# Cross attention's output projections as seven half-size products per weight unit, their weight sums on GpSimd

## The reference, cut to what matters

```
def memory_cross_attention(h, mem, g_mem, w_q, w_kv, w_o):
    ...
    p = jax.nn.softmax(sc, axis=-1)                                   # 4 heads of 256
    o = jnp.einsum("bhqk,bkhd->bqhd", p, v.astype(jnp.float32))
    return o.reshape(b, s, D_MODEL) @ w_o                             # 256x1024 by 1024x1024
h = h + memory_cross_attention(...)
h = h + squared_relu_mlp(rmsnorm(h, ...), ...)
```

## Time and profile before

| what | value |
| --- | --- |
| time, median of three runs | 1585.96 us (1585.59 to 1586.88) |
| the profiled execution: its time | 1585.89 us |
| its span, first to last instruction | 1584.1 us |
| TensorE busy | 1431.3 us, 90% |
| VectorE, ScalarE, GpSimd busy | 765.3, 313.5, 29.9 us |
| granted TensorE clock, mean | 0.962 |

### The profile page before, as it was taken

One profiled execution on the slowest core, in us unless ns is written; L12 is line 12 of the kernel. 1 busy time (PEld: TensorE's weight loads), 2 busy tenths in 40 slices (PEclk: granted clock), 3 DMA queues, 4 the chain that ended last, 5 costly groups with the idle time before them and its releaser, 6 DMA issues.

```text
span 1584.1 us, 23677 instructions
## 1 busy us (share of the span) xinstructions
PE 1431.3 (90%) x10066; PEld 1119.1 (71%) x10066; DVE 765.3 (48%) x1567; ACT 313.5 (20%) x774; POOL 29.9 (2%) x51
## 2 busy tenths in 40 slices
PE   9999999999999999999999999999988566657657
PEld 8779989998888799899988888888743112113113
DVE  6637617879667556178797678823320000000000
ACT  1332022220024520122200343332211000000000
POOL 0000000000002000000000012000000000000000
PEclk9999999999999999999999999999999888787889
DMA  9525415776434054157665204346899999999998
GB/s 394 236 80 192 181 54 192 287 279 265 164 143 181 33 209 164 54 208 289 262 266 225 82 1 132 118 131 262 354 394 426 426 426 429 427 426 428 426 427 346
DMA packets 47625, 396.53 MB, mean 250 GB/s; under 512 B 16416, under 2 KB 20256, under 8 KB 22688
## 3 DMA queue, kind: packets, MB, share of 16 engines
q1 hardware_dynamic: 46048, 393.53, 62.3%
q10 hardware_dynamic: 1472, 1.49, 0.3%
HBM read 392.38 MB, written 2.63 MB: 249 GB/s over the span
## 4 chain that ended last, share of the span: by engine, by line
PE 73%; DMA 22%; DVE 2%; SPq 1%; ACT 1%; issue 0%; ACTq 0%; DVEq 0%
PE pb L542 30%; DMA arena<-in_w_experts 21%; PE pb L1174 12%; PE pb L1138 11%; PE pb L642 7%; PE pb L1049 5%; PE pb L1082 3%; PE pb L1223 2%; SPq L1840 1%; PE pb L977 1%; PE pb L1249 1%; PE pb L713 1%; DMA cols<-in_cols 0%; ACT arena L1904 0%; DVE arena L3178 0%
## 5 line engine op out<-in xcount | busy, mean ns | idle before, releaser
L542 PE MATMUL pb<-hT,ring 128*128 128x256 f32 x768 | 173.2, 382 | 0.2 <-DVE arena L3300 0.2
L542 PEld LDWEIGHTS pb<-hT,ring 128*128 128x128 f32 x768 | 143.5, 190 | 24.9 <-issue 5.9
L542 PE MATMUL pb<-ring,hT 128*32 128x512 f32 (+2 forms) x704 | 110.4, 671 | 43.4 <-DMA ring<-in_w_experts 42.1
L3460 DVE SCALAR_TENSOR_TENSOR side<-side,pb 128x256 f32<-128x256 f32 x16 | 6.7, 422 | 267.3 <-ACT side L1904 267.3
L642 PE MATMUL pb<-arena,ring 128*128 128x256 f32 x512 | 118.2, 382 | 0.0
L1904 ACT ACTIVATE arena<-pb 128x512 f32<-128x512 f32 (+4 forms) x122 | 53.2, 458 | 305.3 <-PE pb L542 116.0
L542 PEld LDWEIGHTS pb<-ring,hT 128*32 128x32 f32 (+1 forms) x704 | 32.6, 131 | 110.1 <-issue 63.2
L642 PEld LDWEIGHTS pb<-arena,ring 128*128 128x128 f32 x512 | 94.9, 190 | 14.6 <-issue 2.9
L1904 ACT ACTIVATE side<-pb 128x256 f32<-128x256 f32 (+2 forms) x58 | 23.1, 407 | 402.1 <-PE pb L542 386.0
L542 PE MATMUL pb<-arena,hT 128*32 128x512 f32 x248 | 41.8, 796 | 34.6 <-DMA arena<-in_w_experts 21.5
L542 PE MATMUL pb<-ring,side 128*32 128x256 f32 (+1 forms) x608 | 45.2, 452 | 20.4 <-DMA ring<-in_w_experts 15.9
(11 more groups left out here) (489 smaller groups left out, 2498.1 us busy)
## 6 DMA issues: line engine op xcount, KB each, us to landing
ring<-in_w_dense SPq DMA_DIRECT2D x85, 2048.0 KB, 8.0
ring<-in_w_experts SPq DMA_DIRECT2D x54, 2048.0 KB, 45.3
arena<-in_w_experts SPq DMA_DIRECT2D x18, 2048.0 KB, 44.6
extra<-in_w_experts SPq DMA_DIRECT2D x9, 2048.0 KB, 45.3
cons<-in_w_experts SPq DMA_DIRECT2D x9, 1024.0 KB, 45.0
arena<-in_w_experts SPq DMA_DIRECT2D x9, 1024.0 KB, 41.9
ring<-in_w_experts SPq DMA_DIRECT2D x4, 1024.0 KB, 6.8
ring<-in_w_dense SPq DMA_DIRECT2D x2, 1536.0 KB, 6.4
```

Of the source, the lines that this page charges most:

```text
L542: return nc.tensor.matmul(o, l, r, start=st, stop=sp)
```

## The change

The output projection of both layers becomes seven half-size products for each of its two weight units. Weight sums T1 to T4 are made by GpSimd, into `extra` and `hT` (T3 in place in the unit), all eight from the moment that q1's last product is done. Row sums are made by VectorE: S3 behind head 2, S1, S2, S4 behind head 3. The products are issued by `out_product`: unit 0's 1 behind `turn(2)`, its 7 ahead of `turn(3)`, unit 1's 1 behind `turn(3)`, its 7 behind the last head, then 2 of both units, then 5, 6, 4, 3 of unit 0 and of unit 1. ScalarE copies product 1 of both units out of PSUM (`first_outs`) ahead of the last head's output. VectorE adds the products to quarters of the residual (`first_quarter`, `other_quarters`). The banks of q1's product become (6, 3, 7). `out_weight` is one subtraction of 128x1024 on GpSimd, `out_row` one sum or difference of 128x512 on VectorE, `first_quarter` adds product 2's bank to the residual's first quarter (128x256); `first_outs` is called in ScalarE's `attention` between the copies of the last head's `t` and `o`.

```
-                cross_columns(layer, "q1", (3, 6, 7), first_scores)
+                cross_columns(layer, "q1", (6, 3, 7), first_scores)
 
                 def all_copied():
-                    open_projection(f"xo{layer}_")
+                    for i in range(2):
+                        out_unit[layer, i] = take()
                     pe.wait_ge(v_ready, 8 * (layer + 1))
                     copied(pe, f"xq1{layer}_0", f"xq1{layer}_1")
 
-                attention(stage, all_copied, lambda h, part: between_cross(stage, h, part))
-                project(5)
+                attention(stage, all_copied, lambda h, part: between_cross(layer, h, part))
+                out_product(layer, 1, "7")
                 copied(pe, *outs(stage))
-                project(6)
-                project(7, final=True)
+                for i in range(2):
+                    out_product(layer, i, "2")
+                for i in range(2):
+                    for x in "5643":
+                        out_product(layer, i, x)
...
+            def out_product(layer, i, x):
+                w, u = out_unit[layer, i]
+                y = [[yT[:, HALF[b_], TOK[t]] for b_ in range(2)] for t in range(TT)]
+                place = {"1": 0, "2": 0, "4": 0, "5": 1, "3": 1, "6": 2, "7": 2}
+                lhs = {"1": w[:, HALF[0], FEAT[0]], "2": w[:, HALF[1], FEAT[0]], "3": w[:, HALF[1], FEAT[1]], "4": ow[i][2],
+                       "5": ow[i][0], "6": ow[i][1], "7": w[:, HALF[0], FEAT[1]]}
+                rhs = {"1": y[0][0], "2": y[0][1], "3": vh[3], "4": y[1][1], "5": vh[0], "6": vh[1], "7": vh[2]}
+                b = ((0, 4, 2), (3, 5, 1))[i][place[x]]
...
+                if x in "4567":
+                    pe.wait_ge(ow_ready, out_weights(layer, i, {"5": "T1", "6": "T2", "7": "T3", "4": "T4"}[x]))
+                if x in "3567":
+                    pe.wait_ge(oh_ready, out_rows(layer, {"5": "S1", "6": "S2", "7": "S3", "3": "S4"}[x]))
+                if x == "2":
+                    pe.wait_ge(op_copied, 2 * layer + i + 1)
+                if x == "4":
+                    pe.wait_ge(o2_read, 2 * layer + i + 1)
+                if x == "3":
+                    pe.wait_ge(o5_read, 2 * layer + i + 1)
+                for f in range(2):
+                    for k in range(4):
+                        o = side_ * S + f * P
+                        last = nc.tensor.matmul(pb[:, b, o:o + P], lhs[x][:, k, f * P:(f + 1) * P], rhs[x][:, k, :],
+                                                start=x in "157" and f == 0 and k == 0, stop=x not in "15" and k == 3,
+                                                skip_group_check=True)
+            def between_cross(layer, h, part):
+                at_ = {(2, 1): (0, "1"), (3, 0): (0, "7"), (3, 1): (1, "1")}
+                if (h, part) == (2, 1):
+                    copied(pe, *(f"o{FIRST_HEAD[f'xa{layer}'] + j}" for j in range(2)))
+                if (h, part) in at_:
+                    out_product(layer, *at_[h, part])
...
+        OUT_WEIGHTS = ((0, "T1"), (0, "T3"), (1, "T1"), (1, "T3"), (0, "T2"), (0, "T4"), (1, "T2"), (1, "T4"))
+            def out_weights_of(layer):
+                b, done = product_done["cross", layer, "q1", "3"]
+                pool.wait_ge(filled[b], done)
+                for i, which in OUT_WEIGHTS:
+                    out_weight(layer, i, which)
...
+            def first_outs(layer):
+                for i in range(2):
+                    b, m = product_done["out", layer, i, "1"]
+                    act.wait_ge(filled[b], m)
+                    fn(out_p1[i], pb[:, b, 0:S], ACT.Copy).then_inc(op_copied, 1)
...
+                    elif h == 2:
+                        copied(dve, *heads_out[0:2])
+                        out_row(layer, "S3")
+                attention(f"xa{layer}", behind_head)
+                copied(dve, *heads_out[2:4])
+                for which in ("S1", "S2", "S4"):
+                    out_row(layer, which)
+                for i in range(2):
+                    first_quarter(layer, i)
+                for i in range(2):
+                    other_quarters(layer, i, lambda c: col(f"mlp_norm{layer}", c))
-                add(f"xo{layer}_", lambda c: col(f"mlp_norm{layer}", c))
+            def other_quarters(layer, i, gain):
+                V.tensor_tensor(x11, x11, product_of(b, 0), ALU.add).then_inc(o5_read, 1)
+                link(V.tensor_tensor(u, u, product_of(b, 0), ALU.add))
+                link(V.tensor_tensor(x10, x10, u, ALU.add))
+                V.tensor_tensor(u, u, product_of(b, 1), ALU.add).then_inc(freed[b], 1)
+                link(V.tensor_tensor(x01, x01, u, ALU.add))
+                link(V.tensor_tensor(x11, x11, u, ALU.add))
+                for f, quarter, x, sign in ((0, x01, "4", ALU.subtract), (1, x10, "3", ALU.add)):
+                    V.tensor_tensor(quarter, quarter, product_of(b, 1 - f), sign).then_inc(freed[b], 1)
+                    V.tensor_scalar(raw(c), xT[:, c, :], gain(c), None, ALU.mult).then_inc(raw_ready, 1)
```

More of the change, by code:

```diff
@@ L426, in program, with out_weights, out_rows @@
         product_done, down_unit, value_unit, up_unit = {}, {}, {}, {}
+        out_unit = {}
+        OUT_WEIGHTS = ((0, "T1"), (0, "T3"), (1, "T1"), (1, "T3"), (0, "T2"), (0, "T4"), (1, "T2"), (1, "T4"))
+        OUT_ROWS = ("S3", "S1", "S2", "S4")
+        def out_weights(layer, i, which):
+            return 8 * layer + OUT_WEIGHTS.index((i, which)) + 1
+        def out_rows(layer, which):
+            return 4 * layer + OUT_ROWS.index(which) + 1
         summed = {}
@@ L676, in between_cd @@
                     project(c, 1 - part, first=c == 0)
[L678 to L683, removed]
+            def out_product(layer, i, x):
[5 more added lines that the diff above has]
+                rhs = {"1": y[0][0], "2": y[0][1], "3": vh[3], "4": y[1][1], "5": vh[0], "6": vh[1], "7": vh[2]}
+                side_ = x in "47"
+                name = f"xo{layer}_{i}_{place[x]}"
+                b = ((0, 4, 2), (3, 5, 1))[i][place[x]]
+                if x in "157":
+                    fill(name, b)
+                if x in "4567":
[14 more added lines that the diff above has]
+                                                skip_group_check=True)
+                mark(last, name, True, u if x == "3" else None)
+                product_done["out", layer, i, x] = (b, marks[b])
@@ L1858, in _, with out_weight @@
         def _(pool):
+            def out_weight(layer, i, which):
+                w, u = out_unit[layer, i]
+                w11, w12, w21, w22 = (w[:, HALF[a_], FEAT[b_]] for a_ in range(2) for b_ in range(2))
+                if which == "T1":
+                    pool.wait_ge(loaded[slot_of[u]], 16 * nth[u])
+                else:
+                    pool.wait_ge(ow_ready, out_weights(layer, i, "T2" if which == "T4" else "T1"))
+                if which == "T1":
+                    ins = nc.gpsimd.tensor_tensor(ow[i][0], w12, w11, ALU.subtract)
+                elif which == "T2":
+                    ins = nc.gpsimd.tensor_tensor(ow[i][1], w22, ow[i][0], ALU.subtract)
+                elif which == "T3":
+                    ins = nc.gpsimd.tensor_tensor(w12, w22, w12, ALU.subtract)
+                else:
+                    ins = nc.gpsimd.tensor_tensor(ow[i][2], ow[i][1], w21, ALU.subtract)
+                ins.then_inc(ow_ready, 1)
+            def out_weights_of(layer):
[3 more added lines that the diff above has]
+                    out_weight(layer, i, which)
+            out_weights_of(0)
             b, done = product_done["mixer", "qd", "3"]
@@ L2653, in cross, with behind_head @@
                 block_12(layer, "q0")
-                def last_queries(h):
+                heads_out = [f"o{FIRST_HEAD[f'xa{layer}'] + j}" for j in range(4)]
+                def behind_head(h):
                     if h == 0:
@@ new lines, in cross, with out_row @@
+                for i in range(2):
+                    first_quarter(layer, i)
+                for i in range(2):
+                    other_quarters(layer, i, lambda c: col(f"mlp_norm{layer}", c))
+            def out_row(layer, which):
+                y11, y12, y21, y22 = (yT[:, HALF[b_], TOK[t]] for t in range(TT) for b_ in range(2))
+                if which in ("S2", "S4"):
+                    dve.wait_ge(oh_ready, out_rows(layer, "S1" if which == "S2" else "S2"))
+                if which == "S1":
+                    ins = V.tensor_tensor(vh[0], y21, y22, ALU.add)
+                elif which == "S2":
+                    ins = V.tensor_tensor(vh[1], vh[0], y11, ALU.subtract)
+                elif which == "S3":
+                    ins = V.tensor_tensor(vh[2], y11, y21, ALU.subtract)
+                else:
+                    ins = V.tensor_tensor(vh[3], y12, vh[1], ALU.subtract)
+                ins.then_inc(oh_ready, 1)
```

32 lines of the change are left out of this document (29 added, 3 removed).

## The result

The change makes the kernel slower: 1596.39 us in the median of four runs (1594.63 to 1600.84) against 1586.28 (a fourth run of it joins the three above), ratio 1.0067, 95% interval 1.0056 to 1.0079. The forecast was 1581.6, its range 1580.0 to 1586.5; the time lies above it, beyond both slow rivals (1591.1 and 1593.8).

The account below looks back on a forecast made before the run. TensorE was taken to bound layers 0 and 1, DMA the end from us 1200. Per layer 2.63 + 0.53 - 0.06 - 0.45 - 0.5 = 2.15, two layers 4.3, from 1585.89 to 1581.6 us; range 1580.0 to 1586.5.

Parts of the forecast that it names:

- both slow rivals: Port held for both scalings of a pair: 1591.1 us, chance 0.13; GpSimd sums late for products: 1593.8, chance 0.03.
- the shared port: Heads 1 and 2: GpSimd sums delay VectorE's SBUF scalings 0.5 us each, 0.45 covered; loss 0.5 us per layer.
- the port is held, and both scalings of a pair are caught: Scalings 1 and 2 wait half a sum, then a whole one: 2.6 us lost per layer, 1591.1 us, chance 0.13.
- The sums' size: GpSimd's 128x1024 weight sums: 1.9 us each, the eighth ending near us 222; the tightest due time allowed 4.3 us.
- The products: Output projection: 14 half-size products of 1.79 us replace eight `project` calls, saving TensorE 2.63 us per layer.
- The bank swap: Behind q1's last product: transposes start at once, scores of head 2 come earlier; gain 0.53 us per layer.
- o1's copy: Product 1 of unit 0 waits for ScalarE's copy of o1 behind `weigh(1)`: loss 0.45 us per layer.
- The seam: From the last products to the MLP: VectorE's adds and scaled chunks are ready in time, nothing lost.
- Without the port: Rival: one-input scalings pass beside GpSimd's sums without waiting; gain 5.3 us, 1580.6 us, chance 0.25.
- the gain carries through to the end: The DMA-saturated stretch from us 1200 moves along with earlier savings; the opposing rival: 1585.9 us, chance 0.04.
- The chances: Summary for the whole kernel: faster by over 0.2% 0.66, within 0.19, slower 0.15.

Follow-up runs that it names:

- the PSUM kernel: The changed kernel with exponentials kept in PSUM, where VectorE's scalings read them, and GpSimd's sums unchanged: 1583.34 us, 0.9982 of the kernel before.
- The two kernels without it: The changed kernel with scalings reading PSUM (1583.34 us), and the changed kernel with all eight weight sums on VectorE (1582.95 us).
- the three kernels: Redundant waits added to the kernel with sums on VectorE (128: 1581.91 us; 256: 1580.19) and to the one with PSUM scalings (128: 1580.72).
- 64 waits: The changed kernel with sums on VectorE, plus 64 redundant waits in TensorE's stream: 1583.05 us, 0.9986 of the kernel before.

## Why the prediction was wrong

**The step that failed is the shared port.** It stood in the sum at 0.5 us per layer ("Sum 2 meets scalings 1 ...: 0.5 late. Sum 4 meets scalings 2: 0.5 late, of which 0.45 was idle"). Measured: 2.98 + 3.05 = 6.0 us of waits per layer, from pairs of scalings that took 3.81 and 3.88 instead of 0.62. That is the rival "the port is held, and both scalings of a pair are caught", given 0.13: mechanism, place and order were right, its price of 2.85 a head was 3.2. The four experiments above show it from four sides: it goes when the scalings leave SBUF as their input, it goes when the sums leave GpSimd, it comes with the sums alone, and it shrinks with the length of GpSimd's instruction.

The mistake lay in reading. There a VectorE operation with two inputs in SBUF took 0.84 for 0.69 beside a running GpSimd scaling, and I took this for the way of the port in general. The same form of VectorE operation, S3, took 2.84 beside a GpSimd sum. So the row was right and told of another GpSimd instruction, one with a single input; from it I chose a value between ends far apart, when the row met this case on neither engine. The second part I had argued and weighed too low: a pair of scalings with a gap between them gives a never-empty GpSimd queue the chance to take the port back, and it took it each time. (S3, issued next, waited for one sum only, which ended at 223.66: S3 ended at 224.22, and the last sum, started at 223.75 beside it, took 2.69.) The Trainium skill, page "SBUF — State Buffer", § Who interferes with whom, states the exclusion for the whole instruction. Beside sums this case's runs agree with it (1.47 and 2.42 us for scalings of 0.35, beside sums of 2.35), apart from the last 0.2 us or so of a sum: the scalings end 0.15 us behind it, and need 0.35 themselves. The 0.84 of the earlier trace rows, beside a one-input scaling, still stands against it, and no run looked at that pair.

**The sums' size.** 1.9 us forecast, 2.35 measured; a straight line through rows of 128 and 512 elements on fewer or as many partitions was too low by a fifth. The estimate of 2.25 from the Trainium skill, page "GPSIMD Engine Reference", § 3.1 (4497 ns for 2048 elements, halved), was nearer. They ended late enough to matter to nobody but the scalings: no product waited for a sum. Their length enters the price of the port, one sum for one scaling: with 1.9 us the same mechanism gave 2.85 a head, with 2.35 it gives half a sum and a whole one, 3.5, near the 3.2 measured.

**The products.** Right. Fourteen of 1.79 us each were forecast; eleven took 19.65, 1.786 each. (14 x 1.79 is 25.06 and not 25.0; at 1.786 it is 25.0.) Less work on TensorE by 2.6 us per layer is in the changed kernel too: waits grew from 0.61 to 6.3, 5.7; less 2.6 is 3.1, and each of the two transpositions that start behind a wait takes 0.66 instead of 0.44 in the chain: 3.5, against 3.43 measured.

**The bank swap.** Forecast 0.53, measured 0.27 in the trace of one pair of kernels and 0.12 in the other, and no time. The step took the scores to start 0.17 us behind the end of `block_12`; they started 0.58 behind it in the swap alone (206.65 + 0.42 = 207.07 against 207.65) and 0.29 in the PSUM kernel. What fills that gap the trace does not say.

**o1's copy** cost 0.30 instead of 0.45, with the sums on VectorE; in the changed kernel it lay under the waits. **The seam** to the MLP had no stall and VectorE's adds were nowhere late, as forecast.

**Without the port** the forecast had 2.65 us per layer, 5.3 in all, 1580.6. The two kernels without it gained 2.26 and 2.35 per layer and ran at 1583; that the gain carries through to the end was right only in part, since the run of small matmuls, its pauses and the lower clock behind them, took 0.8 to 2.6 us of it, and the part behind it about 1. With 128 or 256 waits the three kernels came to 1580.2 to 1581.9. No step of mine had such a term, in either direction; in the changed kernel it is 1.9 us of the 8.7. With 3.43 us lost per layer in place of the rival's 2.6 that makes 1585.89 + 6.86 + 1.9 = 1594.65, and the profiled execution took 1594.63. That it meets so closely is luck: the 0.52 ahead of the stretch and the 0.6 won at the end are left out and cancel. The profiled execution was the fastest of the four; the median lies 1.8 above it, within their scatter of 6 us.

**The chances.** Those given to the rivals add up to 0.18 within 0.2% and 0.16 slower; the summary has 0.19 and 0.15.

## What to carry over

Before work goes to an idle GpSimd, list what VectorE does beside it with input and output in SBUF on the path of TensorE, and price each such instruction at the rest of a running GpSimd instruction, and the next one of a pair at a whole one. If it must lie there, cut GpSimd's instructions small, or let VectorE's small ones read PSUM, or give VectorE the sums: it makes them in half the time and in an order that the program sets. And an edit that changes nothing late in a kernel may still go with other pauses in a dense run of small matmuls there: that run took 47.7 to 52.0 us. So before a difference of 0.2% is put down to the edit, compare the chain's "issue" rows, and the granted clock behind every pause and long wait.

## What the runs showed of the hardware that was not expected

- Which operations GpSimd's sum of 2.35 us holds up: VectorE's scaling from SBUF to SBUF (0.35 alone, 1.47 and 2.42) and its two-input sum in SBUF (S3, 0.69 alone, 2.84). Not: the scaling out of PSUM (0.88 a pair), the row maximum out of PSUM (0.69), the reciprocal of two elements (0.15).
- GpSimd is held up too: its sum took 2.81 when VectorE's S3 had started 0.24 us ahead of it.
- In a dense run of small matmuls TensorE pauses for up to 2.78 us with no releaser. The granted clock is 1.00 ahead of the pause; behind 2.78, 2.51 (sums in pieces), 1.96 and 1.70 us (64 waits) it was 0.50 for some 3 us, behind 2.51 and 2.23 in the two kernels with PSUM scalings it stayed at 1.00. Redundant waits on a set semaphore ahead of the run (128 or 256 of them) shortened it to 47.8 to 48.1 us in five of five kernels, from 49.4 to 52.0. Without a releaser in the trace, the cause stays open.
- Behind a wait of TensorE of 3.01 us the granted clock fell to 0.50 for some 3 us in layer 0, and behind one of 3.0 us in layer 1 of the same execution it stayed at 1.00.
- 32 matmuls of 8 columns in float32 took 9.71 us at the kernel's start: 0.20 us each at a granted clock of 1.00 (us 7 to 11), about 0.4 at 0.50 (us 13 to 17).
